# Column groups of a split-precision projection: two passes of 512 and 256 columns against three of 256

## The chip, the cores and the metric

One NeuronCore of a Trainium2 chip. The metric is the device time of one execution in microseconds (us), from the first to the last instruction of that core and what little lies around it. Engines in the profile: PE is TensorE's matmuls, PEld its weight loads, DVE is VectorE, ACT is ScalarE, POOL is GpSimd, SP is SyncE (here the engine that issues most DMAs).

## What is computed

Two layers of a decoder trunk over 256 tokens of width 2048, all in fp32. Each layer is, with `x` of 256 x 2048:

```python
h = rms_norm(x, pre_norm[i])
proj = h @ w_in[i]                       # 2048 x 7168: token mixer (3 x 1536), memory query 512, gate 2048
if i == 0: tok_out = gate_b * conv3(gate_c * x_in)            # short gated convolution
else:      tok_out = differential causal attention with rotary, 12 heads
cross_out = softmax(q_mem @ km.T / sqrt(128)) @ vm            # 4 heads, km and vm from rms_norm(mem) @ w_kv_mem[i]
branch = concat([tok_out, cross_out]) * silu(gate)
x = x + rms_norm(branch @ w_out[i], post_norm[i])
```

## The kernel before

**Split products.** Every large product is made of three products of float32r halves: an operand a is split into a high half (a rounded copy) and a low half (a minus that copy), and a x b is taken as hi x hi + hi x lo + lo x hi. The inputs stand transposed in SBUF as `X[:, kt, 0:256]` (high) and `X[:, kt, 256:512]` (low), 16 blocks kt of 128 rows: `XA` (trace name hT_split) for the normalised x, `XB` (memT_split) for the memory, `XC` (branchT_split) for the branch.

**Units.** The weights stream through rings of four slots. A unit is 1024 weights in each of 128 partitions, 512 KB. SyncE loads it into `raw` (L215), ScalarE makes the high half `whi` (L588, in `high`), VectorE makes the low half `wlo` (L794, in `low`), TensorE uses both. ScalarE writes a slot once TensorE is through with the unit four before (semaphore unit_done); SyncE refills `raw` once VectorE has made the low half. In `ahead`, ScalarE and VectorE prepare, during one group, the units of the next.

**Two kinds of groups.** A row group (512 weight columns; the inputs are the stationary operand and the weights move) makes rows of tokens: for each input block three matmuls of 512 columns, L367 to L369 (low input x high weights, high x low, high x high). A column group makes 256 columns of the projection, transposed, so that features lie on partitions: the weight tile of 128 x 128 is stationary and the 256 tokens move. It has 4 units; in each unit, for 4 blocks kt and 2 column tiles c, there are two matmuls: the high weights times both halves of the input, 512 columns wide (L340), and the low weights times the high input, 256 wide (L341), added on columns 256 to 511 of the same PSUM bank. So a bank holds the main sum in columns 0 to 255 and the small terms in 256 to 511. There are 54 column groups, of 2 x 16 = 32 weight tiles each. In `matmul(out, stationary, moving)` each matmul brings its own weight load.

**Taking a column group.** When the 4 units are done, ScalarE's `take_small` (L595) copies the small half of two banks, 128 x 512 elements, to `small`; then VectorE's `combine` (L801) adds it to the main half and writes the sum to SBUF, and raises bank_free. Groups alternate between two pairs of banks, and TensorE waits before group G for bank_free of group G - 2 (`first_bank_wait`). Consumers read the sum in SBUF: `tanh_of` (L694) and `silu_twice` (L921) for gates, the products of the convolution (L955 to L971), `scale_keys` for the memory keys, and in layer 1 `swap_halves` (L277) on SyncE's queue, which swaps halves of queries and keys by DMA for the rotary rotation (`rope`, L1064 to L1068).

**Order of the work.** All orders are written out by hand. Layer 0: memory keys (2 column groups), memory values (row group), memory queries (2), cross gates (2), then a loop of 6 mixer steps with 4 column groups each (x_in, gate_c, gate_b, gate), then 4 row groups of the output projection. Layer 1: memory keys (2), values, queries (2), 3 row groups for the attention's values, then 6 pairs of heads with 3 column groups each (query, key, gate), 2 cross gates, and the output projection. The attention of pair p - 1 is laid between the units of pair p: TensorE does the scores (`diff_scores`, L539) after the first unit of the query group, the turn of the weights (L511) and the values (L520 to L522) in the key group, and the turn of the output (`diff_out_turn`, L528) in the gate group, while VectorE and ScalarE do the softmax, the normalisation (`out_norm`, L1076) and the rotation at fixed places between their units. VectorE and ScalarE work strictly in the order written, so a step that waits holds up the low or high halves behind it.

Of the kernel before, what the change touches and what calls it, by code (L numbers as in the profile page):

```python
# [13 lines left out]
P = 128  # L14
# [44 lines left out]

def columns_before(G, row_groups):  # L60

    return G - row_groups


# [17 lines left out]
def build(nc, x_in, mem_in, positions, pre_norm, post_norm, mem_norm, w_in, w_kv_mem, w_out,  # L82
# [24 lines left out]
    small = sb("small_terms", [P, 2, 256])  # L107
# [18 lines left out]
    crossT1 = L1[:, 7168:8192].rearrange("p (h t) -> p h t", h=CROSS_HEADS)  # L126

# [38 lines left out]


# [11 lines left out]
    small_copied = sem("small_copied")  # L179
# [136 lines left out]
    def _(pe):  # L316
# [7 lines left out]
        def column_group(G, u, s, X, x_steps=None, at={}):  # L324
# [3 lines left out]
            for n in range(B_UNITS):  # L328
# [59 lines left out]
        def cross_scores(l):  # L388
            pe.wait_ge(km_ready, l + 1)
# [181 lines left out]
    def _(act):  # L571
# [31 lines left out]

        def column_group(G, u, s, at={}):
            ahead(u, B_UNITS, at)
            take_small(G, u, s)
# [61 lines left out]
        column_group(G_KM0, U_KM0, 0)  # L668
# [6 lines left out]
        column_group(G_KM0 + 1, U_KM0 + B_UNITS, 1)  # L675
# [9 lines left out]
        column_group(G_QM0, U_QM0, 1)  # L685
        for n in range(4):
            turned(N_MEM1 + n, XB, 3 * KT)
        column_group(G_QM0 + 1, U_QM0 + B_UNITS, 0)
# [3 lines left out]
        def tanh_of(G, src, dst):  # L692
            act.wait_ge(bank_free, G + 1)
            run(dst, src, ACT.Tanh, scale=0.5).then_inc(tanh_done, 1)  # L694

        column_group(G_XG0, U_XG0, 1)
        tanh_of(G_XG0, val0, xin)
        cross_exp(0)
        column_group(G_XG0 + 1, U_XG0 + B_UNITS, 0)
        tanh_of(G_XG0 + 1, val0, xin)  # L700
        cross_take(0)
        with act.Fori(0, PAIRS) as j:
            for g in range(4):
                G = j * 4 + (G_MIX + g)
                column_group(G, j * (4 * B_UNITS) + (U_MIX + B_UNITS * g), (G_MIX + g) % 2)
            tanh_of(G, val0, xin)
# [4 lines left out]
        column_group(G_KM1, U_KM1, G_KM1 % 2)  # L711
# [4 lines left out]
        column_group(G_KM1 + 1, U_KM1 + B_UNITS, (G_KM1 + 1) % 2)  # L716
# [7 lines left out]
        column_group(G_QM1, U_QM1, G_QM1 % 2)  # L724
        column_group(G_QM1 + 1, U_QM1 + B_UNITS, (G_QM1 + 1) % 2)
# [36 lines left out]
        def pair(p, s, first=False):  # L762
            G, u = p * 3 + G_PAIR, p * (3 * B_UNITS) + U_PAIR
            column_group(G, u, s, at={} if first else {2: lambda: exps(p - 1)})
            column_group(G + 1, u + B_UNITS, 1 - s,
                         at={} if first else {2: lambda: take_weights(p - 1), 3: lambda: take_values(p - 1)})
            column_group(G + 2, u + 2 * B_UNITS, s)
            tanh_of(G + 2, val1, tanh1)

        pair(0, G_PAIR % 2, first=True)  # L770
        with act.Fori(1, PAIRS - 1, 2) as p:
# [3 lines left out]
        column_group(G_XG1, U_XG1, G_XG1 % 2, at={2: lambda: exps(PAIRS - 1)})  # L775
        tanh_of(G_XG1, val1, tanh1)
        column_group(G_XG1 + 1, U_XG1 + B_UNITS, (G_XG1 + 1) % 2,
                     at={2: lambda: take_weights(PAIRS - 1), 3: lambda: take_values(PAIRS - 1)})
        tanh_of(G_XG1 + 1, val1, tanh1)
# [5 lines left out]
    def _(dve):  # L785
# [24 lines left out]
        def column_group(G, columns, u, s, dst, at={}):  # L810
            ahead(u, B_UNITS, at)
            combine(G, columns, u, s, dst)
# [60 lines left out]
        column_group(G_KM0, 0, U_KM0, 0, kmT[:, 0:2, :])  # L873
# [10 lines left out]
        column_group(G_KM0 + 1, 1, U_KM0 + B_UNITS, 1, kmT[:, 2:4, :], at={0: mem_stat})  # L884
        row = mem_rstd_row.unsqueeze(1).broadcast_to([P, CROSS_HEADS, MEM_LEN])

        def scale_keys(l):

            dve.wait_ge(bank_free, (G_KM0, G_KM1)[l] + 2)
            V_.tensor_tensor(kmT, kmT, row, MULT).then_inc(km_ready, 1)  # L890

        def take_row():
# [3 lines left out]
            scale_keys(0)  # L896
# [11 lines left out]
        column_group(G_QM0, 2, U_QM0, 1, qmT[:, 0:2, :])  # L908
        for n in range(4):
            turned(N_MEM1 + n, XB, 3 * KT)  # L910
        column_group(G_QM0 + 1, 3, U_QM0 + B_UNITS, 0, qmT[:, 2:4, :])
# [25 lines left out]
        column_group(G_XG0, 4, U_XG0, 1, val0)  # L937
        op(silu_twice(1, xin, val0, xgate[:, 0:2, :]))
        cross_max(0)
        cross_normalise(0)  # L940
        column_group(G_XG0 + 1, 5, U_XG0 + B_UNITS, 0, val0)
        op(silu_twice(2, xin, val0, xgate[:, 2:4, :]))


        before_mix, MIX_STEPS = st.n, 11
        with dve.Fori(0, PAIRS) as j:
            st = Steps(dve, dve_step, before_mix + j * MIX_STEPS)
            G, c, u = j * 4 + G_MIX, j * 4 + columns_before(G_MIX, 1), j * (4 * B_UNITS) + U_MIX
# [262 lines left out]
```

## Time and profile before

| | us |
|---|---|
| timed runs | 976.68, 978.41, 983.6 |
| their median | 978.41 |
| span of the profiled execution | 976.1 |
| busy in it: PE | 951.2 |
| PEld | 819.9 |
| DVE | 636.7 |
| ACT | 469.7 |

The profile is one execution taken by the hardware profiler; the span runs from its first to its last instruction, and no other time of that execution is given. Starts of matmuls are recorded, their ends are modelled, so two matmuls in a row are shown overlapping and the distance of their starts is what tells their cost. Weight loads (PEld) overlap the matmuls. Waits are inferred from semaphores.

### The profile page before, as it was taken

Reading aid. Unit: us, or ns where it says so; the run is one execution under the profiler, and the core shown is the slowest. Engines: PE = TensorE matmul, PEld = TensorE weight load, DVE = VectorE, ACT = ScalarE, POOL = GpSimd, SP = SyncE. Lnnn points to the kernel's source line nnn. Section 1 sums busy time; section 2 is a strip of 40 time slices with the busy share of each in tenths; the row PEclk is TensorE's granted clock in tenths of the full one; section 3 lists DMA queues with packets and bytes.
Section 4 is the critical chain, followed back from the end, with each engine's and each line's share of the span. In section 5 each row is a group of like instructions: output and inputs, shape, how many; then the busy total and the mean of one; then the engine's idle time right before and its main releaser. Section 6 shows DMA issues by size and latency. Waiting matters only on the chain.

```text
span 976.1 us, 14093 instructions
## 1 busy us (share of the span) xinstructions
PE 951.2 (97%) x5161; PEld 819.9 (84%) x5161; DVE 636.7 (65%) x894; ACT 469.7 (48%) x708; POOL 1.2 (0%) x9
## 2 busy tenths in 40 slices
PE   6999999999999999999999999999999999999995
PEld 5788888888888888888888888888888888888884
DVE  5776656666666666655685465467877878777555
ACT  5756544444444443444464455446445364454441
POOL 0000000000000000000000000000000000000000
PEclk9999999999999999999999999999999999999998
DMA  9665465566666555656567645565565555746552
GB/s 317 222 230 182 136 210 173 184 203 193 194 191 191 186 186 192 210 186 202 166 230 202 189 141 195 169 204 158 176 190 152 177 167 155 198 151 203 198 177 86
DMA packets 149689, 182.30 MB, mean 187 GB/s; under 512 B 8016, under 2 KB 118928, under 8 KB 148880
## 3 DMA queue, kind: packets, MB, share of 16 engines
q1 hardware_dynamic: 148704, 177.25, 57.7%
q10 hardware_dynamic: 944, 4.49, 1.3%
q8 instruction: 27, 0.44, 0.2%
q14 instruction: 14, 0.11, 0.0%
HBM read 176.48 MB, written 2.10 MB: 183 GB/s over the span
## 4 chain that ended last, share of the span: by engine, by line
PE 71%; DVE 14%; DMA 5%; issue 4%; ACT 3%; SPq 2%; DVEq 0%; ACTq 0%
PE psum L340 27%; PE psum L341 13%; PE psum L369 9%; PE psum L368 9%; PE psum L367 9%; DVE lo_ring L794 5%; DMA layer_area<-layer_area 5%; SPq L277 2%; ACT layer_area L758 2%; PE psum L384 1%; DVE layer_area L801 1%; ACT hi_ring L588 1%; DVE psum L1088 1%; DVE layer_area L1065 1%; DVE columns L1092 1%
## 5 line engine op out<-in xcount | busy, mean ns | idle before, releaser
L340 PE MATMUL psum<-hT_split,hi_ring 128*128 128x512 f32 x1600 | 560.1, 396 | 0.0
L794 DVE TENSOR_TENSOR lo_ring<-raw_ring,hi_ring 128x1024 fp32r<-128x1024 f32 x320 | 386.3, 1223 | 240.5 <-ACT hi_ring L588 237.6
L588 ACT ACTIVATE hi_ring<-raw_ring 128x1024 fp32r<-128x1024 f32 x320 | 337.5, 1062 | 403.4 <-PE psum L341 262.1
L341 PE MATMUL psum<-hT_split,lo_ring 128*128 128x256 f32 x1600 | 445.3, 278 | 0.0
L340 PEld LDWEIGHTS psum<-hT_split,hi_ring 128*128 128x128 f32 x1600 | 300.6, 188 | 68.3
L341 PEld LDWEIGHTS psum<-hT_split,lo_ring 128*128 128x128 f32 x1600 | 301.3, 188 | 0.3
L367 PE MATMUL psum<-hi_ring,branchT_split 128*128 128x512 f32 x256 | 100.0, 391 | 0.0
L369 PE MATMUL psum<-hi_ring,branchT_split 128*128 128x512 f32 x256 | 99.7, 390 | 0.0
L368 PE MATMUL psum<-lo_ring,branchT_split 128*128 128x512 f32 x256 | 99.7, 390 | 0.0
L368 PEld LDWEIGHTS psum<-lo_ring,branchT_split 128*128 128x128 f32 x256 | 48.1, 188 | 10.0
L367 PEld LDWEIGHTS psum<-hi_ring,branchT_split 128*128 128x128 f32 x256 | 48.1, 188 | 9.9
L369 PEld LDWEIGHTS psum<-hi_ring,branchT_split 128*128 128x128 f32 x256 | 48.1, 188 | 9.8
L340 PE MATMUL psum<-memT_split,hi_ring 128*128 128x512 f32 x128 | 45.4, 399 | 1.7 <-DVE lo_ring L794 1.7
L367 PE MATMUL psum<-hi_ring,hT_split 128*128 128x512 f32 x96 | 37.7, 393 | 0.0
L368 PE MATMUL psum<-lo_ring,hT_split 128*128 128x512 f32 x96 | 37.4, 390 | 0.0
L369 PE MATMUL psum<-hi_ring,hT_split 128*128 128x512 f32 x96 | 37.4, 390 | 0.0
L341 PE MATMUL psum<-memT_split,lo_ring 128*128 128x256 f32 x128 | 35.9, 280 | 0.0
L801 DVE TENSOR_TENSOR layer_area<-psum,small_terms 128x512 f32<-128x512 f32 x46 | 31.8, 691 | 3.3
L595 ACT ACTIVATE small_terms<-psum 128x512 f32<-128x512 f32 x54 | 31.6, 584 | 0.0
L340 PEld LDWEIGHTS psum<-memT_split,hi_ring 128*128 128x128 f32 x128 | 24.1, 188 | 7.9 <-issue 2.2
L367 PE MATMUL psum<-hi_ring,memT_split 128*128 128x512 f32 x64 | 25.4, 397 | 0.5 <-DVE lo_ring L794 0.5
L758 ACT ACTIVATE layer_area<-psum,columns 128x128 f32<-128x128 f32 (+1 forms) x48 | 19.4, 430 | 13.1 <-DVE columns L1094 13.1
(159 smaller groups left out, 650.7 us busy)
## 6 DMA issues: line engine op xcount, KB each, us to landing
raw_ring<-in_w_in_dram SPq DMA_DIRECT2D x224, 512.0 KB, 4.4
raw_ring<-in_w_out_dram SPq DMA_DIRECT2D x64, 512.0 KB, 4.8
raw_ring<-in_w_kv_mem_dram SPq DMA_DIRECT2D x32, 512.0 KB, 5.3
layer_area<-layer_area SPq DMA_DIRECT2D x48, 64.0 KB, 4.0
stage_area<-in_mem_dram SPq DMA_DIRECT2D x4, 512.0 KB, 7.5
x_residual<-in_x_dram SPq DMA_DIRECT2D x1, 2048.0 KB, 10.9
x_residual<-in_x_dram ACTq DMA_DIRECT2D x1, 2048.0 KB, 8.6
layer_area<-in_post_norm_dram ACTq DMA_DIRECT2D x2, 1024.0 KB, 6.2
```

The source lines that it names most:

```text
L277: sp.dma_start(dst[32 * b:32 * b + 32, :], src[o:o + 32, :]).then_inc(rot_loaded, 16)
L340: mm(o, hi[:, k, P * c:P * (c + 1)], X[:, kt, :], start=kt == 0, stop=False)
L341: last = mm(o[:, SEQ:], lo[:, k, P * c:P * (c + 1)], X[:, kt, 0:SEQ], start=False, stop=kt == KT - 1)
L367: mm(o, xl, hi[:, k, :], start=first, stop=False)
L368: mm(o, xh, lo[:, k, :], start=False, stop=False)
L369: last = mm(o, xh, hi[:, k, :], start=False, stop=final)
L384: last = nc.tensor.transpose(ps[:, 4 + n % 4, 256 * k + P * t:256 * k + P * (t + 1)], src[:, t, P * kt:P * (kt + 1)], ident)
L588: run(whi[:, slot, :], raw[:, slot, :], ACT.Copy).then_inc(hi_ready, 1)
L595: run(small, banks(s)[:, :, SEQ:], ACT.Copy).then_inc(small_copied, 1)
L758: run(prob[:, h, m, P * t:P * (1 + 2 * t)], (score0 if t == 0 else score1)[:, m, h, :], ACT.Exp, bias=xnegmax[:, i:i + 1], scale=D_SCALE, ...
L794: V_.tensor_tensor(wlo[:, slot, :], raw[:, slot, :], whi[:, slot, :].bitcast(f32), SUB)\
L801: V_.tensor_tensor(dst, banks(s)[:, :, 0:SEQ], small, ADD).then_inc(bank_free, 1)
```

## The change

Column groups now take three 256-wide passes per weight tile, all into columns 0 to 255 of the bank: high weights x high input, high weights x low input, low weights x high input. With the sum complete in PSUM, `take_small`, `combine` and the buffer `small` go. What follows reads PSUM:

- ScalarE copies a finished group to SBUF (`take_columns`) where it is needed there: memory keys of layer 0, memory queries, x_in of the mixer, queries and keys of the pairs (24 groups).
- For the 16 gate groups ScalarE takes the tanh from PSUM (`take_tanh`) and VectorE's `silu_twice` reads the gate from PSUM and frees the banks.
- VectorE's products with gate_c and gate_b in the mixer read PSUM (12 groups), and the memory keys of layer 1 are scaled as they are read (2 groups).

The diff, cut to its core:

```diff
-                        o = banks(s)[:, c, :]
-                        mm(o, hi[:, k, P * c:P * (c + 1)], X[:, kt, :], start=kt == 0, stop=False)
-                        last = mm(o[:, SEQ:], lo[:, k, P * c:P * (c + 1)], X[:, kt, 0:SEQ],
-                                  start=False, stop=kt == KT - 1)
+                        o, part = columns_of(s)[:, c, :], slice(P * c, P * (c + 1))
+                        mm(o, hi[:, k, part], X[:, kt, 0:SEQ], start=kt == 0, stop=False)
+                        mm(o, hi[:, k, part], X[:, kt, SEQ:], start=False, stop=False)
+                        last = mm(o, lo[:, k, part], X[:, kt, 0:SEQ], start=False, stop=kt == KT - 1)
...
+    def columns_of(s):
+        return ps[:, 2 * s:2 * s + 2, 0:SEQ]
...
-        def take_small(G, u, s):
+        def take_columns(G, u, s, dst):

             act.wait_ge(unit_done, u + B_UNITS)
             if not isinstance(G, int) or G >= 1:
                 act.wait_ge(bank_free, G)
-            run(small, banks(s)[:, :, SEQ:], ACT.Copy).then_inc(small_copied, 1)
+            run(dst, columns_of(s), ACT.Copy).then_inc(bank_free, 1)
+
+        def take_tanh(G, u, s, dst):
+
+            act.wait_ge(unit_done, u + B_UNITS)
+            act.wait_ge(bank_free, G)
+            run(dst, columns_of(s), ACT.Tanh, scale=0.5).then_inc(tanh_done, 1)
...
-        def combine(G, columns, u, s, dst):
-
-            dve.wait_ge(lo_ready, u + (SLOTS + B_UNITS))
-            dve.wait_ge(small_copied, columns + 1)
-            V_.tensor_tensor(dst, banks(s)[:, :, 0:SEQ], small, ADD).then_inc(bank_free, 1)
-
+        def columns_done(G, u):
+
+            dve.wait_ge(unit_done, u + B_UNITS)
+            dve.wait_ge(bank_free, G)
...
-        def silu_twice(tanhs, tanh, gate, dst):
+        def silu_twice(tanhs, s, tanh, dst):

             dve.wait_ge(tanh_done, tanhs)
-            return V_.scalar_tensor_tensor(dst, tanh, 1.0, gate, ADD, MULT)
+            V_.scalar_tensor_tensor(dst, tanh, 1.0, columns_of(s), ADD, MULT).then_inc(bank_free, 1)
...
-            mixer_group(0, xin)
-            mixer_group(1, val0)
-            st.did(V_.tensor_tensor(upad[:, :, 2:], val0, xin, MULT))
-            st.need()
+            ahead(u, B_UNITS, {})
+            ahead(u + B_UNITS, B_UNITS, {})
+            columns_done(G + 1, u + B_UNITS)
+            V_.tensor_tensor(upad[:, :, 2:], xin, columns_of((G_MIX + 1) % 2), MULT).then_inc(bank_free, 1)
+            dve.wait_ge(bank_free, G + 2)
...
-            mixer_group(2, val0)
-            st.did(V_.tensor_tensor(conv, conv, val0, MULT))
-            mixer_group(3, val0)
-            st.did(silu_twice(j + 3, xin, val0, val0))
-            st.need()
-            st.did(V_.scalar_tensor_tensor(val0, val0, 0.5, conv, MULT, MULT))
+            ahead(u + 2 * B_UNITS, B_UNITS, {})
+            columns_done(G + 2, u + 2 * B_UNITS)
+            V_.tensor_tensor(conv, conv, columns_of(G_MIX % 2), MULT).then_inc(bank_free, 1)
+            ahead(u + 3 * B_UNITS, B_UNITS, {})
+            silu_twice(j + 3, (G_MIX + 3) % 2, val0, val0)
+            dve.wait_ge(bank_free, G + 4)
+            st.did(V_.scalar_tensor_tensor(conv, val0, 0.5, conv, MULT, MULT))
...
-        scale_keys(1)
+        for i, at in enumerate(({1: lambda: add_y(0), 2: lambda: add_y(1)}, {2: lambda: scale_x(4, y_all)})):
+            ahead(U_KM1 + B_UNITS * i, B_UNITS, at)
+            columns_done(G_KM1 + i, U_KM1 + B_UNITS * i)
+            V_.tensor_tensor(kmT[:, 2 * i:2 * i + 2, :], columns_of((G_KM1 + i) % 2), row[:, 0:2, :], MULT)\
+              .then_inc(bank_free, 1)
...
-            column_group(G, c, u, s, two(qT), at=in_query)
-            column_group(G + 1, c + 1, u + B_UNITS, 1 - s, two(kT), at=in_keys)
-            column_group(G + 2, c + 2, u + 2 * B_UNITS, s, val1, at=in_gate)
-            dve.wait_ge(bank_free, G + 3)
-            st.did(silu_twice(p + (PAIRS + 3), tanh1, val1, sgate[parity]))
+            ahead(u, B_UNITS, in_query)
+            ahead(u + B_UNITS, B_UNITS, in_keys)
+            ahead(u + 2 * B_UNITS, B_UNITS, in_gate)
+            silu_twice(p + (PAIRS + 3), s, tanh1, sgate[parity])
```

The cross gates change in the same way as the mixer's gates. TensorE no longer waits for km_ready before the cross scores of layer 1; the wait for bank_free of the queries covers it. `out_take` and `cross_branch` get a wait for an earlier step of VectorE itself.

## Rows read from the trace of the kernel before

**Rows 1.** Head of the page: span, busy time, the granted clock in 40 slices
```profile
span 976.1 us, 14093 instructions
PE 951.2 (97%) x5161; PEld 819.9 (84%) x5161; DVE 636.7 (65%) x894; ACT 469.7 (48%) x708; POOL 1.2 (0%) x9
...
PEclk9999999999999999999999999999999999999998
```

**Rows 2.** Part 5 of the page: costliest groups; busy, mean ns, idle before
```profile
L340 PE MATMUL psum<-hT_split,hi_ring 128*128 128x512 f32 x1600 | 560.1, 396 | 0.0
...
L341 PEld LDWEIGHTS psum<-hT_split,lo_ring 128*128 128x128 f32 x1600 | 301.3, 188 | 0.3
...
L340 PE MATMUL psum<-memT_split,hi_ring 128*128 128x512 f32 x128 | 45.4, 399 | 1.7 <-DVE lo_ring L794 1.7
...
L801 DVE TENSOR_TENSOR layer_area<-psum,small_terms 128x512 f32<-128x512 f32 x46 | 31.8, 691 | 3.3
L595 ACT ACTIVATE small_terms<-psum 128x512 f32<-128x512 f32 x54 | 31.6, 584 | 0.0
```

**Rows 3.** Windows; us of PE, PEld, DVE, ACT, POOL, then granted clock, DMA share, GB/s
```profile
130.00:370.00 240.00, 240.00 (x1387) 209.87 (x1386) 153.31 (x175) 104.81 (x114) 0.00 (x0) 1.00 0.60 188
640.00:870.00 230.00, 225.65 (x1339) 198.27 (x1338) 176.09 (x287) 114.80 (x239) 0.00 (x0) 1.00 0.57 171
```

**Rows 4.** Waits of the weight loads: us in total, times, longest us
```profile
PEld psum L539 <- issue: 3.7, 4, 1.6
PEld psum L528 <- DVE layer_area L1076: 2.8, 3, 0.9
...
PEld psum L445 <- DVE cross_gate L882: 1.3, 1, 1.3
```

**Rows 5.** Chain of waits in one pair: start us, us, what
```profile
710.15 0.70 DVE layer_area L801
...
711.43 0.58 SPq L277
...
712.69 4.34 DMA layer_area<-layer_area
...
717.66 0.70 DVE layer_area L1065
```

**Rows 6.** Line L340, 150 to 350 us: count, first and last start
```profile
L340 PE MATMUL psum<-hT_split,hi_ring x578: 392/394/396, 149.8 to 349.8; 128*128 128x512 f32 x193
```

**Rows 7.** Line L368 in the output row groups: count, first and last start
```profile
L368 PE MATMUL psum<-lo_ring,branchT_split x122: 388/390/390, 391.9 to 474.2; 128*128 128x512 f32 x122
```

**Rows 8.** Timeline of TensorE in a row group: start us, us
```profile
520.75 0.39 PE L368 MATMUL psum<-lo_ring,memT_split 128*128 128x512 f32 x1
520.98 0.39 PE L369 MATMUL psum<-hi_ring,memT_split 128*128 128x512 f32 x1
521.21 0.39 PE L367 MATMUL psum<-hi_ring,memT_split 128*128 128x512 f32 x1
```

**Rows 9.** Timeline of TensorE in the mixer stretch: start us, us
```profile
300.23 0.39 PE L340 MATMUL psum<-hT_split,hi_ring 128*128 128x512 f32 x1
300.46 0.28 PE L341 MATMUL psum<-hT_split,lo_ring 128*128 128x256 f32 x1
300.58 0.40 PE L340 MATMUL psum<-hT_split,hi_ring 128*128 128x512 f32 x1
```

**Rows 10.** Timeline of the weight loads beside it: start us, us
```profile
300.46 0.19 PEld L340 LDWEIGHTS psum<-hT_split,hi_ring 128*128 128x128 f32 x1
```

**Rows 11.** Line L401, turns of the cross weights
```profile
L401 PEld LDWEIGHTS psum<-ident,stage_area x16: 138/140/144, 116.0 to 117.7; 128*128 128x128 f32 x16
```

**Rows 12.** Timeline: the last matmul
```profile
965.33 0.39 PE L369 MATMUL psum<-hi_ring,branchT_split 128*128 128x512 f32 x1
```

**Rows 13.** Line L1064, first product of a rotation: durations, what it waited for
```profile
L1064 DVE TENSOR_TENSOR layer_area<-layer_area,sinT x12: 692/693/695, 639.1 to 849.2; 128x512 f32<-128x512 f32 x12
...
  DMA layer_area<-layer_area: 25.7, 12
```

More of the change, by code:

```diff
@@ L126, in build, with two @@
     crossT1 = L1[:, 7168:8192].rearrange("p (h t) -> p h t", h=CROSS_HEADS)
+    def two(ap):
+        return ap.rearrange("p (c t) -> p c t", c=2)
     def l1(at):
@@ L667, in _ @@
                 high(0, n // 2 + 1, n // 2)
-        column_group(G_KM0, U_KM0, 0)
+        ahead(U_KM0, B_UNITS, {})
+        take_columns(G_KM0, U_KM0, 0, kmT[:, 0:2, :])
         for t in range(TT):
@@ L674, in _ @@
             squares(mem_raw[:, t, :], gpost, ss[:, t:t + 1], mem_squared)
-        column_group(G_KM0 + 1, U_KM0 + B_UNITS, 1)
+        ahead(U_KM0 + B_UNITS, B_UNITS, {})
+        take_columns(G_KM0 + 1, U_KM0 + B_UNITS, 1, kmT[:, 2:4, :])
         act.wait_ge(x_loaded, 16)
@@ L684, in _ @@
         act.dma_start(xres, x_in[0].rearrange("(t p) d -> p t d", p=P)).then_inc(x_loaded, 16)
-        column_group(G_QM0, U_QM0, 1)
+        ahead(U_QM0, B_UNITS, {})
+        take_columns(G_QM0, U_QM0, 1, qmT[:, 0:2, :])
         for n in range(4):
             turned(N_MEM1 + n, XB, 3 * KT)
-        column_group(G_QM0 + 1, U_QM0 + B_UNITS, 0)
+        ahead(U_QM0 + B_UNITS, B_UNITS, {})
+        take_columns(G_QM0 + 1, U_QM0 + B_UNITS, 0, qmT[:, 2:4, :])
         for n in range(4, 8):
             turned(N_MEM1 + n, XB, 3 * KT)
[L692 to L697, printed above, removed]
+        ahead(U_XG0, B_UNITS, {})
+        take_tanh(G_XG0, U_XG0, 1, val0)
         cross_exp(0)
-        column_group(G_XG0 + 1, U_XG0 + B_UNITS, 0)
-        tanh_of(G_XG0 + 1, val0, xin)
+        ahead(U_XG0 + B_UNITS, B_UNITS, {})
+        take_tanh(G_XG0 + 1, U_XG0 + B_UNITS, 0, val0)
         cross_take(0)
         with act.Fori(0, PAIRS) as j:
[L703 to L706, printed above, removed]
+            G, u = j * 4 + G_MIX, j * (4 * B_UNITS) + U_MIX
+            ahead(u, B_UNITS, {})
+            take_columns(G, u, G_MIX % 2, xin)
+            ahead(u + B_UNITS, B_UNITS, {})
+            ahead(u + 2 * B_UNITS, B_UNITS, {})
+            ahead(u + 3 * B_UNITS, B_UNITS, {})
+            take_tanh(G + 3, u + 3 * B_UNITS, (G_MIX + 3) % 2, val0)
         act.wait_ge(branch_ready, PAIRS + 1)
@@ L710, in _ @@
             out_group(g, U_OUT0 + A_UNITS * g, (G_OUT0 + g) % 2)
-        column_group(G_KM1, U_KM1, G_KM1 % 2)
+        ahead(U_KM1, B_UNITS, {})
         for t in range(TT):
@@ L723, in _ @@
            .then_inc(late_loaded, 16)
-        column_group(G_QM1, U_QM1, G_QM1 % 2)
-        column_group(G_QM1 + 1, U_QM1 + B_UNITS, (G_QM1 + 1) % 2)
+        for i in range(2):
+            ahead(U_QM1 + B_UNITS * i, B_UNITS, {})
+            take_columns(G_QM1 + i, U_QM1 + B_UNITS * i, (G_QM1 + i) % 2, qmT[:, 2 * i:2 * i + 2, :])
         def tables():
@@ L763, in pair @@
             G, u = p * 3 + G_PAIR, p * (3 * B_UNITS) + U_PAIR
[L764 to L768, printed above, removed]
+            ahead(u, B_UNITS, {} if first else {2: lambda: exps(p - 1)})
+            take_columns(G, u, s, two(qT))
+            ahead(u + B_UNITS, B_UNITS,
+                  {} if first else {2: lambda: take_weights(p - 1), 3: lambda: take_values(p - 1)})
+            take_columns(G + 1, u + B_UNITS, 1 - s, two(kT))
+            ahead(u + 2 * B_UNITS, B_UNITS, {})
+            take_tanh(G + 2, u + 2 * B_UNITS, s, tanh1)
         pair(0, G_PAIR % 2, first=True)
@@ L872, in _ @@
                 low(0, n // 2 + 1, n // 2)
-        column_group(G_KM0, 0, U_KM0, 0, kmT[:, 0:2, :])
+        ahead(U_KM0, B_UNITS, {})
         def mem_stat():
```

83 lines of the change are left out of this document (33 added, 50 removed).

## The prediction

> **What bounds the kernel now.** I read the head of the page first [rows 1]: TensorE is busy 97% of a span of 976.1 us at the full granted clock, VectorE 65%, ScalarE 48%. A busy matmul row says little, because the ends of matmuls are modelled, so I went on to the pace at which they start. In the mixer stretch (130 to 370 us) TensorE is never idle and VectorE has work for 153 of 240 us [rows 3]: there nothing but the pace of the passes counts. The stretch of the attention pairs (640 to 870 us) has the only other pattern: TensorE lacks 4.35 us, and VectorE is at 176 of 230 us. The table of waits for the weight loads names the places [rows 4]: the attention scores (L539) and the turn of the attention output (L528) lose 3.7 and 2.8 us, and the memory norm in the opening (L445) 1.3 us. The chain of waits in that stretch does not run on TensorE but through VectorE and the swap transfer [rows 5]: low halves (L794), the sum of a column group (L801), SyncE's four issues (L277), 4.34 us of transfer, the rotation (L1065). So over the kernel TensorE's own pace is the bound, with some 8 us of gaps on top that VectorE's lateness opens.
>
> **What a pass costs now.** A weight tile in a column group takes one 512-wide and one 256-wide pass. From its first to its last record in the mixer stretch L340 starts 578 times in 200.0 us, over 577 intervals: 346.6 ns for a tile [rows 6]. In the row groups three 512-wide passes repeat: L368 starts 122 times from 391.9 to 474.2 us, which is 82.3 / 121 = 680.2 ns, or 226.7 ns a pass [rows 7]. Let a pass cost a per column plus b fixed. Then 768a + 2b = 346.6 and 1536a + 3b = 680.2. Twice the first less the second gives b = 13.0 ns, and a = (346.6 - 26.0) / 768 = 0.4174 ns, which is 2.396 columns a nanosecond, the upper of the two clock levels, as the granted clock of 1.00 says [rows 3]. That the slope comes out at the clock is what makes me trust the split. The 13.0 ns come with every pass, and also where the same stationary tile is used twice running: L368 and L369 both take the high half of the input as stationary operand, each has its own load, and their starts are as far apart, 0.23 us, as across a change of tile [rows 8]. So the second high pass will not get a cheaper start for having the same weights.
>
> **The change, part by part.** (1) Three 256-wide passes instead of 512 + 256. The columns are the same 768. The passes go from two to three for each of 1600 + 128 = 1728 tiles [rows 2], so 768a + 3b = 320.6 + 39.0 = 359.6 ns, 13.0 more, and 1728 x 13.0 = 22.5 us, all on the bounding engine. No 256-wide pass that follows a 256-wide one stands in this trace, so I bound it. From below: the starts in the mixer stretch go 230 and 116 ns apart in turn [rows 9], so if a 256-wide pass really costs those 116 ns, three cost 348, and the change adds about 1 ns, or nothing. From above: a load that nothing hides would show its whole 188 ns [rows 2], three of them 564 ns. I take 359.6, since it is the fit through both kinds of group and lies near the lower bound; the rows nearest to the new pattern are near it too. A load under a 256-wide pass is there already: L340's load starts at 300.46, with the L341 pass, and its own pass starts at 300.58 [rows 9, 10]. The loads of the L401 turns follow each other 16 times in 1.7 us, 113 ns apart [rows 11]. So a load fits into the 120 ns that a new pass lasts, with little to spare.
>
> On this the Trainium skill speaks twice. The page "TensorE: Matmul & The Clock Gate", section "Back-to-back issue gap", has N / 2.4 + 2.5 ns for a pass; by it the third pass would add 2.5 ns a tile, an estimated 4.3 us in all, where the rows here have 13.0 ns. The same page, under "What overlaps and what doesn't", says that a load overlaps running matmuls only when it goes to other row groups, and gives a load about P / 1.2, 107 ns for 128 columns. By that rule, which speaks against this change, each added load would stand exposed, 107 x 1728 = 185 us as an estimate; the trace disagrees already in the kernel before, where a 512-wide pass with its load takes 226.7 ns.
>
> (2) The 54 sums on VectorE go (L801, 0.69 us each) and so do ScalarE's 54 copies of the small half (L595, 0.58 us) [rows 2]. ScalarE gets 24 copies of finished columns to SBUF instead; 16 tanhs and 16 SiLU steps, and 14 products on VectorE, read PSUM where they read SBUF. VectorE loses about 37 us and ScalarE (54 - 24) x 0.58 = 17 us. On the path of the end nearly nothing of it lies: in the mixer stretch TensorE has no idle time at all to give back [rows 3]. (Product steps that read PSUM may be longer or shorter by a little; the sum out of PSUM took 0.69 us and so does a rotation product of the same size in SBUF [rows 2, 13], so I take no difference, and VectorE's idle third covers any.)
>
> (3) Hold of the banks. A group's banks are now kept until its last consumer has read them, and TensorE waits before group G only for group G - 2. Before, VectorE freed them after its last low half and the sum, 710.15 + 0.70 in [rows 5]; now ScalarE's copy, or the product that stands at the same place, does. There is a whole group, 32 x 0.36 = 11.5 us, between. Cost nothing; were this cover gone, each wait would be about a copy long, 0.6 us.
>
> (4) The gaps. In the pairs VectorE's chain gets 0.7 us shorter at each of three groups, query and key columns are in SBUF after one ScalarE copy, and TensorE arrives later by 96 x 13.0 = 1.2 us a pair. The gaps at L539 and L528 are 3.7 us in 4 and 2.8 us in 3 places, so 0.9 us each [rows 4]: I take them as gone. SyncE's swap still has to pass the loads queued ahead of it, which wait for VectorE's low halves, so the swap moves by at most the 0.7 us. In the opening, TensorE reaches its wait for the memory norm (L445, 1.3 us) 64 tiles, 0.8 us, later. Together 3.7 + 2.8 + 0.8 = 7.3; I take 7. The bounds are 0 and 8, the three waits of [rows 4] in full. What is late next is TensorE itself.
>
> (5) The rest: one keys-scaling pass of layer 1 becomes two that read PSUM, a wait on it goes, and the steps after the last column group are not touched: the last 10 us after the last matmul stay [rows 12].
>
> **The sum.** 976.1 + 22.5 - 7 = 991.6 us of span. The page gives no other time of the profiled execution; the median of the timed runs, 978.4, is 2.3 us above the span, the lowest (976.7) 0.6. With 2.3 added: 994 us, 1.6% over the median. Something under 1% either way can't be told from no change with three runs spread over 0.7%.
>
> **The rivals.** A: a 256-wide pass costs its 116 ns and not 120, because what lengthens a pass goes by its columns. For it: the alternating starts, 230 and 116, stand in exactly the ratio 2 to 1 [rows 9]. Against it: then three 512-wide passes should take 694 ns, and they take 680 [rows 7]. The place is every tile; its price is 3 x 116 - 346.6 = 1.4 ns at most and likely 0, and with the 7 us of part 4 the kernel ends at 976.1 + 0 to 2 - 7 = 969 to 971, or 971 to 974 as a median: not slower. It decides from where a new pass is below 116.9 ns, since 1728 x (3 x 116.9 - 346.6) = 7 us. Should a pass following one of equal width be cheaper still, the time falls below 969; nothing shown speaks for that. The 2.5 ns of the skill's section "Back-to-back issue gap" would put the kernel in this rival's band, and share its chance.
>
> B: the load, or the feeding of instructions, becomes the pace. Now four PE instructions are issued in 347 ns; after, six in 360. For it: loads are shown 188 ns long and TensorE's load row is busy 84% [rows 1, 2], and no row sustains one load every 120 ns for more than 16. Against it: loads already start 116 ns apart and overlap [rows 10]. It decides from 120 ns a load; each ns over it costs 1728 x 3 = 5.2 us, so at 125 ns 1020 us, at 130 1046. Its far end, an added load wholly exposed with the 188 ns of its record, is 1728 x 0.188 = 325 us more, some 1300 us, with a chance of under 0.01 within B. That end is what the skill's section "What overlaps and what doesn't" describes.
>
> C: the passes cost what I say, but the gaps stay, since the chain of [rows 5] is kept by the transfer (4.3 us) and not by the sums. For it: VectorE waits 25.7 us for the swaps [rows 13]. Against: TensorE comes later by itself. Time 976.1 + 22.5 + 2.3 = 1001. A part of my own case, and its upper end.
>
> **How the numbers follow.** My forecast with C, 988 to 1001: 0.76 (C 0.10 of it). A: 0.18. B: 0.06. Predicted 994. Faster by over 1% (under 968.6) needs A with a cheaper pass than any seen, 0.04; within 1% (968.6 to 988.2) holds the rest of A and a fixed part of 10 ns or less, 0.17; slower 0.79. My own case alone would run from 988 to 1001. Cutting off at 988 would leave out A and B, 0.24 and more, so the range goes down to 972, inside A's band, and ends at 1001.
>
> **What would show it.** Right: tiles 359 to 361 ns apart in the mixer stretch, three passes of even spacing at 120 ns, TensorE still 97% busy or more, no L801-like sum, gaps before scores and output turns below 2 us in all. Wrong: tiles at 347 ns (A), tiles over 365 ns with loads evenly spaced (B), or gaps as large as before at the two places (C). A granted clock under 1.00 in the mixer stretch would upset the whole working.

## The result and the profile after

The changed kernel takes 991.83 us (median of 4 runs, 990.67 to 992.68) where the kernel before takes 978.58 (4 runs, 976.68 to 983.60). The ratio is 1.012, with a 95% interval of 1.0084 to 1.0155: slower by 1.2%, little but clear of no change. The medians are 13.3 us apart; the profiled executions have spans of 976.1 and 990.9 us, 14.8 apart.

The head and the costliest groups of the page of the changed kernel, to be held against [rows 1, 2]:

```profile
span 990.9 us, 17376 instructions
PE 972.0 (98%) x6889; PEld 918.2 (93%) x6889; DVE 600.9 (61%) x841; ACT 455.5 (46%) x678; POOL 1.2 (0%) x9
...
L588 ACT ACTIVATE hi_ring<-raw_ring 128x1024 fp32r<-128x1024 f32 x320 | 338.4, 1061 | 485.4 <-PE psum L341 342.5
L339 PE MATMUL psum<-hT_split,hi_ring 128*128 128x256 f32 x1600 | 455.8, 285 | 0.0
L341 PE MATMUL psum<-hT_split,lo_ring 128*128 128x256 f32 x1600 | 452.7, 283 | 0.0
L340 PE MATMUL psum<-hT_split,hi_ring 128*128 128x256 f32 x1600 | 452.6, 283 | 0.0
L340 PEld LDWEIGHTS psum<-hT_split,hi_ring 128*128 128x128 f32 x1600 | 307.0, 192 | 0.3
```

The passes of a tile are now L339 to L341, 256 columns each, and there are 1728 more of them and of their loads: 6889 against 5161. TensorE is at 98%, its loads at 93%. The sum (L801) and the copy of the small half (L595) are gone, VectorE lost 36 us of work and ScalarE 14, and the end came later.

The tile's pace in the mixer stretch, where nothing else can matter: first the count of L339 with its first and last start (us), then a stretch of TensorE's timeline (start us, us):

```profile
L339 PE MATMUL psum<-hT_split,hi_ring x556: 283/283/283, 149.9 to 349.7; 128*128 128x256 f32 x186
```
```profile
304.31 0.28 PE L339 MATMUL psum<-hT_split,hi_ring 128*128 128x256 f32 x1
304.43 0.28 PE L340 MATMUL psum<-hT_split,hi_ring 128*128 128x256 f32 x1
304.55 0.28 PE L341 MATMUL psum<-hT_split,lo_ring 128*128 128x256 f32 x1
304.67 0.28 PE L339 MATMUL psum<-hT_split,hi_ring 128*128 128x256 f32 x1
```

There are 556 starts in 199.8 us, so 360.0 ns a tile (before: 346.6, [rows 6]). The starts come every 120 ns without the alternation of [rows 9]. That is the price of the change against this trace, in one number: 13.4 ns for each tile.

The chain that ended last, by engine, first before and then after:

```profile
PE 71%; DVE 14%; DMA 5%; issue 4%; ACT 3%; SPq 2%; DVEq 0%; ACTq 0%
```
```profile
PE 96%; DVE 2%; issue 1%; ACT 1%; DMA 0%; DVEq 0%; ACTq 0%
PE psum L339 21%; PE psum L340 21%; PE psum L341 21%; PE psum L367 9%; PE psum L366 9%; PE psum L368 9%; PE psum L539 2%; PE psum L383 1%; PE psum L409 1%; PE psum L392 1%; DMA cross_gate<-in_mem_norm_dram 0%; PE psum L511 0%; PE psum L401 0%; DVE memT_split L825 0%; DVE x_residual L1160 0%
```

The waits of the weight loads after the change (us in total, times, longest), against [rows 4]:

```profile
PEld psum L419 <- issue: 6.2, 1, 6.2
PEld psum L339 <- issue: 2.5, 2, 1.6
PEld psum L383 <- DVE x_residual L907: 1.5, 1, 1.5
PEld psum L383 <- DMA stage_area<-in_mem_dram: 0.4, 1, 0.4
```

The chain, which before ran for much of the pair stretch through VectorE and the swap transfer [rows 5], now lies on TensorE for 96% of the span, where it had 71%. The waits before the scores, the output turns and the memory norm (3.7, 2.8 and 1.3 us) are not in the list any more. In the windows the pair stretch has TensorE busy throughout, where it lacked 4.35 us [rows 3]:

```profile
130.00:370.00 240.00, 240.00 (x2002) 240.00 (x2002) 130.77 (x143) 94.21 (x95) 0.00 (x0) 1.00 0.61 182
640.00:870.00 230.00, 230.00 (x1898) 228.90 (x1897) 163.25 (x259) 111.67 (x220) 0.00 (x0) 1.00 0.60 176
```

### The profile page after: what moved, and what is told of

Its sections match the earlier page's. It is cut to its first block, busy times and chain, and to the rows that moved or that the text cites. A ratio compares the mean times of both kernels' runs of the same rounds, so it can differ in the third digit from the quotient of the medians.

```text
span 990.9 us, 17376 instructions
## 1 busy us (share of the span) xinstructions
PE 972.0 (98%) x6889; PEld 918.2 (93%) x6889; DVE 600.9 (61%) x841; ACT 455.5 (46%) x678; POOL 1.2 (0%) x9
## 4 chain that ended last, share of the span: by engine, by line
PE 96%; DVE 2%; issue 1%; ACT 1%; DMA 0%; DVEq 0%; ACTq 0%
PE psum L339 21%; PE psum L340 21%; PE psum L341 21%; PE psum L367 9%; PE psum L366 9%; PE psum L368 9%; PE psum L539 2%; PE psum L383 1%; PE psum L409 1%; PE psum L392 1%; DMA cross_gate<-in_mem_norm_dram 0%; PE psum L511 0%; PE psum L401 0%; DVE memT_split L825 0%; DVE x_residual L1160 0%
## 5 line engine op out<-in xcount | busy, mean ns | idle before, releaser
L339 PE MATMUL psum<-hT_split,hi_ring 128*128 128x256 f32 x1600 | 455.8, 285 | 0.0
L341 PE MATMUL psum<-hT_split,lo_ring 128*128 128x256 f32 x1600 | 452.7, 283 | 0.0
L340 PE MATMUL psum<-hT_split,hi_ring 128*128 128x256 f32 x1600 | 452.6, 283 | 0.0
L340 PEld LDWEIGHTS psum<-hT_split,hi_ring 128*128 128x128 f32 x1600 | 307.0, 192 | 0.3
L339 PEld LDWEIGHTS psum<-hT_split,hi_ring 128*128 128x128 f32 x1600 | 306.9, 192 | 0.3
L341 PEld LDWEIGHTS psum<-hT_split,lo_ring 128*128 128x128 f32 x1600 | 306.9, 192 | 0.0
L368 PE MATMUL psum<-hi_ring,branchT_split 128*128 128x512 f32 x256 | 99.6, 389 | 0.0
L368 PEld LDWEIGHTS psum<-hi_ring,branchT_split 128*128 128x128 f32 x256 | 48.1, 188 | 10.0
L339 PE MATMUL psum<-memT_split,hi_ring 128*128 128x256 f32 x128 | 37.4, 292 | 1.9 <-DVE lo_ring L802 1.9
L368 PE MATMUL psum<-hi_ring,hT_split 128*128 128x512 f32 x96 | 37.4, 389 | 0.0
L340 PE MATMUL psum<-memT_split,hi_ring 128*128 128x256 f32 x128 | 37.0, 289 | 0.0
L341 PE MATMUL psum<-memT_split,lo_ring 128*128 128x256 f32 x128 | 36.9, 289 | 0.0
L339 PEld LDWEIGHTS psum<-memT_split,hi_ring 128*128 128x128 f32 x128 | 25.4, 198 | 2.5 <-issue 2.5
L340 PEld LDWEIGHTS psum<-memT_split,hi_ring 128*128 128x128 f32 x128 | 25.4, 198 | 0.0
```

What stands on the lines that cost most here:

```text
L339: mm(o, hi[:, k, part], X[:, kt, 0:SEQ], start=kt == 0, stop=False)
L340: mm(o, hi[:, k, part], X[:, kt, SEQ:], start=False, stop=False)
L341: last = mm(o, lo[:, k, part], X[:, kt, 0:SEQ], start=False, stop=kt == KT - 1)
L368: last = mm(o, xh, hi[:, k, :], start=False, stop=final)
```

## The experiments

**Do the passes alone cost it, and where do the 8 us come from?** The kernel before with nothing but three passes:

```diff
-                        mm(o, hi[:, k, P * c:P * (c + 1)], X[:, kt, :], start=kt == 0, stop=False)
+                        mm(o[:, 0:SEQ], hi[:, k, P * c:P * (c + 1)], X[:, kt, 0:SEQ], start=kt == 0, stop=False)
+                        mm(o[:, SEQ:], hi[:, k, P * c:P * (c + 1)], X[:, kt, SEQ:], start=False, stop=False)
                         last = mm(o[:, SEQ:], lo[:, k, P * c:P * (c + 1)], X[:, kt, 0:SEQ],
```

> The kernel before with three 256-wide passes a tile, but with the small terms still in their own half bank, copied by ScalarE and added by VectorE as before: the passes alone. Both theories: tiles 360 ns apart in the mixer stretch (before 346.6). They part on the 8 us that came back in the changed kernel. If VectorE's and ScalarE's relief gave them, they do not come back here: the waits before scores and output turns stay near 6 us and the span is 976.1 + 23 = 999 us. If they came back because TensorE arrives later at each meeting point, they come back here too: waits under 2 us, span 991 to 993 us.

Measured: 992.86 us (4 runs), ratio 1.0128 (1.008 to 1.0176), span 991.5. The old taking with its 54 copies and 54 sums is all there, and the time is that of the changed kernel. The waits of its weight loads:

```profile
PEld psum L420 <- issue: 6.3, 1, 6.3
PEld psum L340 <- issue: 2.5, 2, 1.7
PEld psum L385 <- DVE x_residual L905: 1.6, 1, 1.6
...
PEld psum L540 <- issue: 0.3, 1, 0.3
```

Of the 6.5 us before scores (here L540) and output turns 0.3 is left. So TensorE's later arrival is enough by itself to close the gaps. What VectorE's relief adds to that is 0.6 us by the two spans (991.5 and 990.9) and 1.0 by the medians (992.86 and 991.83, measured at different times).

**The taking alone.** The changed kernel with passes of 512 and 256 columns:

```diff
-                        o, part = columns_of(s)[:, c, :], slice(P * c, P * (c + 1))
-                        mm(o, hi[:, k, part], X[:, kt, 0:SEQ], start=kt == 0, stop=False)
-                        mm(o, hi[:, k, part], X[:, kt, SEQ:], start=False, stop=False)
-                        last = mm(o, lo[:, k, part], X[:, kt, 0:SEQ], start=False, stop=kt == KT - 1)
+                        o, part = banks(s)[:, c, :], slice(P * c, P * (c + 1))
+                        mm(o, hi[:, k, part], X[:, kt, :], start=kt == 0, stop=False)
+                        last = mm(o[:, SEQ:], lo[:, k, part], X[:, kt, 0:SEQ], start=False, stop=kt == KT - 1)
```

> The changed kernel with its old passes of 512 and 256 columns: the taking from PSUM alone. Left out: the two small terms, which stay in the unread half of the bank. Tiles 347 ns apart. If the relief of VectorE gives the gaps back, the span is 990.9 - 23 = 968 us, with the waits of TensorE at scores and output turns below 1 us. If TensorE's lateness gave them back, the waits return and the span is 974 to 976 us.

Measured: 972.77 us (10 runs) against 977.92, ratio 0.9935 (0.9906 to 0.9964), span 971.1. Its waits:

```profile
PEld psum L418 <- issue: 5.6, 1, 5.6
PEld psum L339 <- issue: 1.9, 2, 1.0
...
PEld psum L538 <- issue: 0.4, 1, 0.4
```

The wait before the scores (L538) is down to 0.4 us and that before the output turns is gone. So the relief, too, is enough by itself. The two causes I had set against each other are both real, and either one closes the same gaps; together they do not give twice as much. (Here "relief" is the whole new taking: less work, and a shorter chain. The last runs below part the two.) The span came out 3 us above the 968 that I expected from it, for two reasons: a tile did not everywhere cost 346.6 ns with two passes, see below, and the opening took longer, so that the third column group starts 1.5 us later than before.

**Does it matter that two passes in a row have the same stationary tile?** The changed kernel with the last two passes of a tile exchanged:

```diff
-                        mm(o, hi[:, k, part], X[:, kt, SEQ:], start=False, stop=False)
-                        last = mm(o, lo[:, k, part], X[:, kt, 0:SEQ], start=False, stop=kt == KT - 1)
+                        mm(o, lo[:, k, part], X[:, kt, 0:SEQ], start=False, stop=False)
+                        last = mm(o, hi[:, k, part], X[:, kt, SEQ:], start=False, stop=kt == KT - 1)
```

> The changed kernel with the passes of a tile in the order high x high, low x high, high x low, so that no two passes in a row have the same stationary tile. If the fixed 13 ns belong to every pass, whatever its weights: 360 ns a tile, span 991 within 1 us. If a repeated stationary tile makes the second pass cheaper or dearer: a tile differs by 5 ns or more, 9 us over the kernel, and the three starts are no longer evenly spaced.

Measured, in one execution: span 990.9 us, the same to the tenth, and 556 starts in 199.8 us as in the changed kernel. The order plays no part.

**How near was the load (rival B)?** The low pass in two passes of 128 columns:

```diff
-                        last = mm(o, lo[:, k, part], X[:, kt, 0:SEQ], start=False, stop=kt == KT - 1)
+                        mm(o[:, 0:P], lo[:, k, part], X[:, kt, 0:P], start=False, stop=False)
+                        last = mm(o[:, P:], lo[:, k, part], X[:, kt, P:SEQ], start=False, stop=kt == KT - 1)
```

> The changed kernel with the low pass cut into two passes of 128 columns: the same columns, one more pass and one more load a tile. If a pass costs 0.417 ns a column and 13 ns, and nothing else bounds it: 2 x 120 + 2 x 66.4 = 373 ns a tile, 13 more, span 990.9 + 1728 x 0.013 = 1013 us. If the load or the issue of instructions is close behind, at somewhere from 107 to 120 ns a pass: 2 x 120 + 2 x (107 to 120) = 454 to 480 ns a tile, span 1150 to 1200 us.

Measured, in one execution: 1172.0 us, span 1170.2. The weight loads, first over the mixer stretch, then one by one:

```profile
L339 PEld LDWEIGHTS psum<-hT_split,hi_ring x432: 192/192/192, 149.8 to 349.5; 128*128 128x128 f32 x144
```
```profile
300.08 0.19 PEld L340 LDWEIGHTS psum<-hT_split,hi_ring 128*128 128x128 f32 x1
300.20 0.19 PEld L341 LDWEIGHTS psum<-hT_split,lo_ring 128*128 128x128 f32 x1
300.32 0.19 PEld L342 LDWEIGHTS psum<-hT_split,lo_ring 128*128 128x128 f32 x1
300.43 0.19 PEld L339 LDWEIGHTS psum<-hT_split,hi_ring 128*128 128x128 f32 x1
300.55 0.19 PEld L340 LDWEIGHTS psum<-hT_split,hi_ring 128*128 128x128 f32 x1
```

A tile takes 199.7 / 431 = 463 ns, in the band of the bound load, and the loads stand nearly evenly 116 ns apart (0.11 to 0.12 us), whether the pass above them has 256 columns or 128. So in this pattern the passes came, on average, no faster than one load of 128 columns in 116 ns, and the changed kernel with 120 ns a pass was 4 ns from it. The long passes did not keep their 120 ns either, or the tile would have taken 2 x 120 + 2 x 116 = 472 ns: once loads set the pace, slope and fixed part no longer hold.

**Load or feeding?** The same four passes, but the two short ones bring only 64 stationary columns each:

```diff
                         mm(o, hi[:, k, part], X[:, kt, 0:SEQ], start=kt == 0, stop=False)
-                        mm(o, hi[:, k, part], X[:, kt, SEQ:], start=False, stop=False)
-                        last = mm(o, lo[:, k, part], X[:, kt, 0:SEQ], start=False, stop=kt == KT - 1)
+                        mm(o[0:64, 0:P], lo[:, k, P * c:P * c + 64], X[:, kt, 0:P], start=False, stop=False)
+                        mm(o[0:64, P:], lo[:, k, P * c + 64:P * c + P], X[:, kt, P:SEQ], start=False, stop=False)
+                        last = mm(o, hi[:, k, part], X[:, kt, SEQ:], start=False, stop=kt == KT - 1)
```

> The run with the cut low pass (464 ns a tile, loads evenly 116 ns apart) again with four passes a tile, but the two short ones (128 columns) load only 64 stationary columns each. Left out: three quarters of the low x high terms. If the pace of that run was set by the columns that the loads bring, these loads take about half and the passes are the bound again: 2 x 120 + 2 x 66 = 373 ns a tile, span 1013 us within 10. If the pace was set by the feeding of instructions, whatever they load: 464 ns again, span 1170 us.

Measured, in one execution: 1075.57 us, span 1073.8. Loads over the mixer stretch and one by one:

```profile
L339 PEld LDWEIGHTS psum<-hT_split,hi_ring x493: 191/191/192, 149.9 to 349.9; 128*128 128x128 f32 x165
```
```profile
300.45 0.13 PEld L340 LDWEIGHTS psum<-hT_split,lo_ring 128*64 128x64 f32 x1
300.57 0.14 PEld L341 LDWEIGHTS psum<-hT_split,lo_ring 128*64 128x64 f32 x1
300.63 0.19 PEld L342 LDWEIGHTS psum<-hT_split,hi_ring 128*128 128x128 f32 x1
300.74 0.19 PEld L339 LDWEIGHTS psum<-hT_split,hi_ring 128*128 128x128 f32 x1
300.86 0.14 PEld L340 LDWEIGHTS psum<-hT_split,lo_ring 128*64 128x64 f32 x1
```

A tile takes 200.0 / 492 = 406.5 ns: neither number. With as many instructions a tile as in the run before it is 57 ns faster, so the feeding of instructions did not set that pace; the columns that the loads bring did, or else the number of rows that the short passes write, which this run halves too. It does not reach 373. In the lines above the loads start 0.12, 0.06, 0.11 and 0.12 us apart: only one of the four steps is short, since a full load follows the second half load and the next full load comes 0.11 us after that. As an estimate, each step may be taken as the longer of the pass and of the load that follows it, with 120 and 66 ns for long and short passes and 116 for a full load. That gives 120 + 66 + 116 + 120 = 422 ns, 15 more than measured: nearer than 373 or 464, but not an account of every ns.

**A version that beats both.** If either cause closes the gaps, they can be closed with two passes. The kernel before, with the small half copied and the sum made ahead of the last high and low halves of the next group, and the swaps ahead of SyncE's last load of a group:

```diff
         def column_group(G, u, s, at={}):                       # ScalarE
-            ahead(u, B_UNITS, at)
-            take_small(G, u, s)
+            ahead(u, B_UNITS - 1, at)
+            if B_UNITS - 1 in at:
+                at[B_UNITS - 1]()
+            take_small(G, u, s)
+            high(u + SLOTS, B_UNITS, B_UNITS - 1)
...
         def column_group(G, columns, u, s, dst, at={}):         # VectorE
-            ahead(u, B_UNITS, at)
-            combine(G, columns, u, s, dst)
+            ahead(u, B_UNITS - 1, at)
+            if B_UNITS - 1 in at:
+                at[B_UNITS - 1]()
+            combine(G, columns, u, s, dst)
+            low(u + SLOTS, B_UNITS, B_UNITS - 1)
... (in combine, VectorE)
-            dve.wait_ge(lo_ready, u + (SLOTS + B_UNITS))
+            dve.wait_ge(lo_ready, u + (SLOTS + B_UNITS - 1))
... (in pair, SyncE)
-                column_group(p * (3 * B_UNITS) + (U_PAIR + B_UNITS * g), w_in[1], p * BCOLS + col)
+                at = {}
                 if g == 0 and not first:
-                    swap_halves(p * 3 + (G_PAIR - 2), kT, krot)
-            swap_halves(p * 3 + G_PAIR, qT, qrot)
+                    at = {3: lambda: swap_halves(p * 3 + (G_PAIR - 2), kT, krot)}
+                if g == 2:
+                    at = {3: lambda: swap_halves(p * 3 + G_PAIR, qT, qrot)}
+                column_group(p * (3 * B_UNITS) + (U_PAIR + B_UNITS * g), w_in[1], p * BCOLS + col, at=at)
```

> The kernel before, two passes and all terms kept, with the small half copied and the sum made before the last high and low half of the next group's units, and with the swap transfers ahead of the last load on SyncE's queue. Nothing of VectorE's work goes; only its place moves. If what the changed kernel gave back came from the reach of the chain sum, swap, rotation (and not from the amount of work on VectorE), the waits at scores and output turns fall below 1 us here too, and the span is 976.1 - 5 to 7 = 969 to 971 us, the median 0.5 to 0.7% under that of before: better than both kernels. If the amount of work is what counts, the waits stay and the span is 975 to 977 us.

Measured: 971.95 us (8 runs) against 978.92, ratio 0.9912 (0.9882 to 0.9943). The waits at the scores and output turns are gone, and so is VectorE's wait for the swap transfers (25.7 us before, [rows 13]). But the profiled execution was one of the two long ones, 977.62 us with a span of 975.8, which looked like the other answer; six of the eight took 970.42 to 972.21. It was run a second time, unchanged.

> The kernel with the early taking and early swaps once more, unchanged, beside the paired order on one chip. Median 970 to 974 us, single executions from 970 to 978. If the pace of a stretch is drawn anew in each execution, this trace has the mixer stretch at 347 or 353 ns a tile, and the span tells which: 970 us with 347, 976 with 353.

Measured: 971.77 us (6 runs, 970.29 to 972.50) against 978.43, ratio 0.9922 (0.9895 to 0.9949), span 970.1. The head of the two-pass tiles over 150 to 350 us, first in the execution with 975.8, then in that with 970.1, and last in the kernel before in the memory keys of layer 1 (476 to 496 us):

```profile
L342 PE MATMUL psum<-hT_split,hi_ring x567: 395/398/403, 149.9 to 349.9; 128*128 128x512 f32 x189
```
```profile
L342 PE MATMUL psum<-hT_split,hi_ring x578: 392/394/395, 149.9 to 349.9; 128*128 128x512 f32 x193
```
```profile
L340 PE MATMUL psum<-memT_split,hi_ring x58: 394/399/404, 475.7 to 495.8; 128*128 128x512 f32 x58
```

That is 200.0 / 566 = 353.4 ns, 200.0 / 577 = 346.6 ns and 20.1 / 57 = 352.6 ns. A two-pass tile has two paces, one of them 6 to 7 ns longer, and keeps one through a stretch. The memory keys and queries of layer 1 have the longer one in every trace of the order 512, 256; the mixer loop has the shorter in the kernel before, and either one in the two executions here. Over the 768 tiles of the mixer loop that is 5.2 us of the 5.7 between the two spans. Both come from the same code, so a single execution of a two-pass kernel settles no difference of a few us: the 19 executions of the kernel before that were timed beside this version spread over 10.6 us (975.73 to 986.29). The two three-pass kernels with four executions each stay within 2.0 and 2.3 us.

The same without moving the swaps:

> As the run before, but the swaps stay behind the last load on SyncE's queue, which waits for the low half that now comes after the sum. If the swap's start is what counts, little is won: the last low half comes 0.6 us later and the swap with it: span 975 to 978 us. If the place of the sum on VectorE alone counts: 970 to 972 us.

Measured: 975.85 us (10 runs) against 978.92, ratio 0.9957 (0.9929 to 0.9984), span 974.7. By the medians it gains about half as much, with intervals that overlap. VectorE still waits 20.8 us for the swaps here. The trace says more than the medians: the head of the two-pass tiles in the mixer stretch, then those from the first pair to the end of the column groups, in this run and in the kernel before:

```profile
L340 PE MATMUL psum<-hT_split,hi_ring x567: 395/398/403, 149.9 to 349.9; 128*128 128x512 f32 x189
```
```profile
L340 PE MATMUL psum<-hT_split,hi_ring x640: 391/392/580, 624.4 to 876.3; 128*128 128x512 f32 x160
```
```profile
L340 PE MATMUL psum<-hT_split,hi_ring x640: 390/392/586, 619.0 to 877.7; 128*128 128x512 f32 x160
```

The last 640 tiles take 251.9 us here and 258.7 before. With the swaps moved they take 251.9 as well, in both executions (625.4 to 877.3 and 619.8 to 871.7). So in the traces the early sum alone brings back the whole 6.8 us, and moving the swaps adds nothing. The 4.6 us between the spans of 974.7 and 970.1 are no more than the 5.2 that the longer pace of the mixer loop makes, and at equal pace this version is not behind (974.7 against 975.8). Whether the difference of the medians, 3.9 us, is also one of paces, executions without a trace cannot show. The engines' work is the same as before in this version, so to close the gaps it is enough to move the copy and the sum ahead in the order of ScalarE and VectorE, without less work and without an earlier swap.

**Are the two paces due to the alternation of long and short passes?** The version with early sum and early swaps, with two neighbouring tiles in the order 512, 512, 256, 256:

```diff
                     for c in range(2):
-                        o = banks(s)[:, c, :]
-                        mm(o, hi[:, k, P * c:P * (c + 1)], X[:, kt, :], start=kt == 0, stop=False)
-                        last = mm(o[:, SEQ:], lo[:, k, P * c:P * (c + 1)], X[:, kt, 0:SEQ],
+                        mm(banks(s)[:, c, :], hi[:, k, P * c:P * (c + 1)], X[:, kt, :], start=kt == 0, stop=False)
+                    for c in range(2):
+                        last = mm(banks(s)[:, c, SEQ:], lo[:, k, P * c:P * (c + 1)], X[:, kt, 0:SEQ],
                                   start=False, stop=kt == KT - 1)
```

> The run with the early taking and early swaps, with the passes of two neighbouring tiles in the order 512, 512, 256, 256 in place of 512, 256, 512, 256. In the traces so far two-pass tiles run at one of two paces, 347 or 353 ns, that hold for a whole stretch, while three-pass tiles always take 360. If the second pace comes from the alternation of long and short passes, two tiles take 693 ns in every stretch, the executions spread less than the 7 us of that run, and the median falls to 970 or 971 us. If the two paces have nothing to do with the order, both still occur: median 972, spread 6 us. If two short passes in a row make the load late, two tiles take over 700 ns everywhere and the span is above 980 us.

Measured: 973.20 us (8 runs, 972.72 to 973.83), ratio 0.9944 (0.9923 to 0.9965), span 970.9. The 512-wide passes in the mixer stretch, then in the memory keys of layer 1:

```profile
L341 PE MATMUL psum<-hT_split,hi_ring x575: 393/395/398, 150.0 to 349.9; 128*128 128x512 f32 x192
```
```profile
L341 PE MATMUL psum<-memT_split,hi_ring x55: 389/395/398, 476.0 to 494.8; 128*128 128x512 f32 x55
```

That is 199.9 / 574 = 348.3 ns and 18.8 / 54 = 348.1 ns a tile: one pace in both stretches, where the order 512, 256 has 353 in the second. Two tiles take 697 ns, not the 693 of the expectation, and the median is not better. All eight executions lie within 1.1 us, against 7.2 us over the eight of the other order in its first run; but its six beside this run spread over 2.2 only, so the spread is weak evidence. The even pace points to the alternation of long and short passes; what in the alternation makes two paces is not shown.

## Why the prediction was right

The predicted 994 us was 2 above the 991.8 measured. Of the span it was 0.7 above (991.6 against 990.9); the rest is the 2.3 us put between span and median, where the profiled execution of the changed kernel took 1.8 us more than its span and was 0.9 longer than the median. The price of a pass and the return of the gaps, which carry the sum, both happened as told.

- **The price of a pass.** Forecast 359.6 ns a tile, measured 360.0; the fit of a slope and a fixed part through two kinds of group held for the third. What the fixed part consists of no run showed. I had 13.0 ns for the third pass; by the rows it is 13.4. Over 1728 tiles that is 23.2 us, but not all tiles cost 346.6 before: the 160 of the memory keys and queries of layer 1 and of the first memory queries of layer 0 took about 353, which takes about 1 us off. I had treated one stretch's pace as that of all.
- **Some luck in the fit.** The trace had the mixer stretch at the shorter of its two paces. At 353.4 ns the same two equations give b = 26.6 ns and a = 0.391, and a forecast of 380.0 ns for a tile that measured 360.0. The slope would have warned: 2.56 columns a nanosecond is above the 2.4 of the clock. And against an execution at the longer pace the third pass costs 6.6 ns a tile in the mixer loop, not 13.4, so the distance between the two kernels changes by 5 us with the execution it is measured from.
- **A row that was there.** I wrote that no 256-wide pass follows a 256-wide one in the trace. There are such rows, the cross attention's (L392 and L409), 16 passes at a time:

```profile
L409 PE MATMUL psum<-stage_area,vm x16: 377/380/380, 384.1 to 387.4; 128*128 128x256 f32 x16
```

They start about 0.22 us apart, nearly twice the 120 ns forecast. Their operands (`kmT`, `qmT`, `vm`) are plain fp32 and not float32r halves, so they were no measure of the new pass, but they had to be named and set aside: at their pace a tile would have taken some 650 ns. The turns of [rows 11] and their 113 ns a load are plain fp32 too, and so spoke less for the new loads than I made of them.
- **Same weights twice.** No cheaper, as [rows 8] had it, and shown by the exchanged order.
- **The gaps.** Forecast 7 us back, from the profiled execution before to that after; the waits of [rows 4] with 7.8 us went, and 0.5 us came on in the opening (5.7 to 6.2 us before the first matmul; no instruction of the change lies ahead of that). 23.2 - 1 - 7.8 + 0.5 = 14.9 us, where 14.8 was measured; other waits moved by under 1 us in both directions. I named two causes, the relief and the lateness, and added them up in the text as if both were needed; each is enough. I had the chain through the swap transfer as what made VectorE late; the early copy and sum, with the swaps left in their place, closed the gaps as well.
- **The relief of VectorE and ScalarE** (forecast 37 and 17 us) measured 36 and 14 us and brought nothing that lateness would not have brought.
- **Rival A** (116 ns a pass) fell with the evenly spaced starts at 120 ns. The 116 ns between two starts was not the cost of the pass between them; the sum of the two distances is what the fit could use. (The estimate of 4.3 us for all third passes, put into the same sum, gives a median of 975.7 us, a little above the 971 to 974 of the band in which I put it.)
- **Rival B** did not happen, but the margin that I called "little to spare" was 4 ns of 120. A fourth pass, with the same columns in all, cost 1170.2 - 990.9 = 179 us, where the passes' own price would have been 23, as the cut pass shows.
- **Rival C** did not happen: the gaps closed, also where the swaps kept their place and the sums were all made (the old taking with three passes, and the early sum alone).

## What to carry to other kernels

Split a series of matmul starts into a cost per column and a fixed cost per pass by two groups of different widths, over long stretches; here the result carried over to a pattern that the trace does not have, down to where the weight load becomes the pace. On an engine that is busy 97% of the time, a change that takes 50 us of work from its helpers and adds 13 ns to each of its own 1728 tiles loses; ask first what the helpers' lateness costs (here 8 us) and whether moving one of their steps earlier gets it back without any added work (here 6 to 7 of 978 us). And look for a second pace before trusting a pace from one stretch: a fitted slope that does not come out at the clock is a sign of it.

## What was not expected of the hardware

- With four passes a tile, weight loads of 128 float32r columns followed each other every 116 ns and set the pace, though each is shown 188 to 192 ns long; with 64 columns in two of four loads a tile went from 463 to 406.5 ns. It is no floor for every load: those of the attention's values (L520 to L522, plain fp32, 128 columns) come 0.11 us apart in the kernel before. The Trainium skill gives P / 1.2, 107 ns for 128 columns ("TensorE: Matmul & The Clock Gate", section "LDWEIGHTS (loading the stationary operand)"): near, and 9 ns short of the 116 here.
- Two-pass tiles (512 + 256 columns) ran at 346.6 or 353.4 ns in the same stretch of the same code, and changed between executions; three equal passes always took 360.0. In the order 512, 512, 256, 256 a tile took 348 ns in both stretches looked at. The cause is open.
